# Expert stage of a streaming encoder layer: the weights stream past stationary activations as fp32r parts, and GpSimd loads x

## What is computed

```python
def expert_block(args):
    xblk, e = args
    hdn = jax.nn.silu(xblk @ w_gate_e[e]) * (xblk @ w_up_e[e])
    return hdn @ w_down_e[e]
```

## Time and profile before

| | |
|---|---|
| median of 3 runs | 2809.85 us (2809.2 to 2811.21) |
| profiled execution | 2812.55 us, span 2811.0 us |
| PE busy | 2419.6 us, 86% |
| PE weight loads | 1997.4 us, 71% |
| DVE busy | 888.5 us, 32% |
| ACT busy | 640.4 us, 23% |
| POOL busy | 168.7 us, 6% |
| HBM read, written | 301.60 MB, 74.39 MB |

### The profile page before, as it was taken

The page is one execution under the profiler, slowest core; times in us unless marked ns, Lnnn a source line. Parts: engine busy times, 40 slices in busy tenths (PEclk is TensorE's granted clock), DMA queues, the critical chain, the costliest instruction groups (busy, mean ns, idle before and its releaser), DMA issues. The chain is left out here.

```text
span 2811.0 us, 38540 instructions
## 1 busy us (share of the span) xinstructions
PE 2419.6 (86%) x14272; PEld 1997.4 (71%) x14272; DVE 888.5 (32%) x1415; ACT 640.4 (23%) x1073; POOL 168.7 (6%) x175
## 2 busy tenths in 40 slices
PE   4678979888797988899999599899279999999992
PEld 3566867667686766899888499845168877888772
DVE  5345354544535453211456432111400000000003
ACT  3133232332322221211465331111000101101010
POOL 0111010110101000000111100000200000000002
PEclk9888999999999975899999899999589999999996
DMA  3211120202111010310555431150568888888875
GB/s 90 59 39 32 46 77 0 77 1 77 31 46 55 0 55 4 121 45 28 150 177 165 139 103 45 52 193 0 187 217 327 309 318 326 326 327 314 313 291 201
DMA packets 237268, 376.83 MB, mean 134 GB/s; under 512 B 17840, under 2 KB 125656, under 8 KB 237176
## 3 DMA queue, kind: packets, MB, share of 16 engines
q1 hardware_dynamic: 216008, 302.26, 31.6%
q0 software_dynamic: 17600, 61.18, 6.8%
q10 hardware_dynamic: 3584, 12.58, 1.1%
HBM read 301.60 MB, written 74.39 MB: 134 GB/s over the span
## 5 line engine op out<-in xcount | busy, mean ns | idle before, releaser
L1715 PEld LDWEIGHTS e_gate_ps<-e_xT,e_gate 128*128 128x128 f32 x2048 | 236.0, 194 | 17.1 <-issue 17.1
L1715 PE MATMUL e_gate_ps<-e_xT,e_gate 128*128 128x96 f32 x2048 | 235.5, 276 | 1.1 <-DVE e_xT L1752 1.1
L1715 PE MATMUL e_up_ps<-e_xT,e_up 128*128 128x96 f32 x2048 | 233.9, 275 | 0.0
L1715 PEld LDWEIGHTS e_up_ps<-e_xT,e_up 128*128 128x128 f32 x2048 | 231.3, 192 | 0.0
L1726 PE MATMUL e_y_ps<-e_down,e_hT 128*96 128x512 f32 x512 | 227.4, 597 | 0.0
L1763 DVE TENSOR_TENSOR e_hT<-e_act,e_up_ps 128x384 f32<-128x384 f32 x32 | 17.7, 553 | 649.4 <-PE e_up_ps L1715 649.4
L1252 DVE COPY probsT<-turn_ps 128x512 f32<-128x512 f32 (+4 forms) x232 | 131.5, 567 | 249.0 <-PE turn_ps L1022 225.0
L101 PE MATMUL proj_ps<-w_qkv_hi,xh 128*128 128x384 f32 x544 | 194.3, 357 | 9.3 <-PEq L285 9.3
L1042 PEld LDWEIGHTS out_ps<-v_new,probsT 128*128 128x128 f32 x1152 | 156.9, 207 | 61.5 <-DVEq L84 45.0
L1152 ACT ACTIVATE probs_s<-scores,neg_max 128x256 f32<-128x256 f32 (+7 forms) x128 | 95.1, 743 | 445.6 <-DVEq L84 445.1
L1042 PE MATMUL out_ps<-v_new,probsT 128*128 128x64 f32 x1152 | 177.1, 294 | 21.2 <-DVEq L84 20.2
(11 more groups left out here) (344 smaller groups left out, 4093.2 us busy)
## 6 DMA issues: line engine op xcount, KB each, us to landing
e_gate<-w_gate_e SPq DMA_DIRECT2D x32, 2048.0 KB, 9.3
e_up<-w_up_e SPq DMA_DIRECT2D x32, 2048.0 KB, 15.1
e_down<-w_down_e SPq DMA_DIRECT2D x32, 2048.0 KB, 13.5
slot_x<-zrows POOLq DMA_DIRECT2D x48, 440.0 KB, 6.4
e_x<-slot_x SPq DMA_DIRECT2D x33, 384.0 KB, 13.0
w_qkv<-w_in SPq DMA_DIRECT2D x24, 512.0 KB, 9.8
slot_y<-e_y ACTq DMA_DIRECT2D x32, 384.0 KB, 6.1
slot_y<-zrows POOLq DMA_DIRECT2D x24, 352.0 KB, 9.6
```

Source lines behind the costliest of these rows:

```text
L1715: last = te.matmul(out[:, f * CAP:(f + 1) * CAP], weights[u][:, k, f * P:(f + 1) * P], xT[:, k, :], start=(k == 0), stop=(k == KT - 1))
```

## The change

The weights of an expert are now loaded as 6 pieces of 1 MiB, 128 x 2048 values: pieces 0 and 1 are gate, 2 and 3 up, 4 and 5 down. Each has one raw buffer. ACT rounds each piece into a high part (`high`), DVE subtracts to get the low part (`low`), both into a ring of 3 slots, and PE multiplies each piece with 12 matmuls of 512 columns (4 slices, three products each) with x or the hidden values as the stationary operand, in parts too. The gate and up results now lie as rows by hidden columns, so the hidden values are turned on PE (4 transposes, `turn_h`) before the down product. The order of the pieces on ACT, DVE and PE is 0, 1, 2, 3 of block b, then 4, 5 of block b-1. SP issues only the weight loads: a piece of the next block when the piece in the same raw buffer has been split. x and y have one buffer each. The load of x is issued by GpSimd on its own queue, after it has waited for the turn of the x before it. A loop body is one block, where it was two.

The loads of the second set of weights in `route` are gone with `second`, all 6 pieces of the first expert are loaded in `merge`. The gate and up sources are read as two rows together, 4 KiB for a partition, and x is turned in the column order that fits this. The semaphores of `normalize` and `forget_gates` come from a stack that is closed before `attend`, and SP clears each of them once at the start of `attend`.

```diff
-                w.load_in(sp, g, 0, 0)
-                w.load_down(sp, g, 0, 0)
+                for c in range(PIECES):
+                    w.load(sp, g, c, 0)
...
-                w.load_in(sp, g, 1, 1)
-                w.load_down(sp, g, 1, 1)
...
+PIECES, PIECE, RING = 6, 2048, 3
...
+        self.raw = [ctx.enter_context(nc.sbuf_tensor(f"e_raw{c}", [P, PIECE], F32)) for c in range(PIECES)]
+        self.loaded = [g.sem(f"e_loaded{c}") for c in range(PIECES)]
+    def load(self, sp, g, c, e):
+        half = slice(c % 2 * 2, c % 2 * 2 + 2)
+        if c < 4:
+            w = (g.w_gate_e, g.w_up_e)[c // 2]
+            src = w[0, bass.ds(e, 1)].rearrange("o (a p b) n -> p (o a) (b n)", p=P, b=2)[:, half, :]
+        else:
+            src = g.w_down_e[0, bass.ds(e, 1)].rearrange("o (a p) n -> p (o a) n", p=P)[:, half, :]
+        sp.dma_start(self.raw[c][:, :].rearrange("p (a n) -> p a n", a=2), src).then_inc(self.loaded[c], 16)
...
+        xb = sb("x", [CAP, D])
+        x_hi, x_lo = sb("xT_hi", [P, KT, CAP], F32R), sb("xT_lo", [P, KT, CAP], F32R)
...
+        w_hi, w_lo = ([sb(f"w_{part}{u}", [P, PIECE], F32R) for u in range(RING)] for part in ("hi", "lo"))
...
             @block.sync
             def _(sp):
                 n = sp.value_load(passes[0:1, 0:1], **limits)
-                def load_x(b, u):
-                    sp.dma_start(xb[u][:, :], g.slot_x[bass.ds(b * CAP, CAP), :]).then_inc(x_loaded[u], 16)
-                load_x(0, 0)
-                load_x(1, 1)
-                with sp.Fori(0, n - 1) as i:
-                    for u in range(2):
-                        b = i * 2 + u
-                        e = sp.value_load(expert_of[0:1, bass.ds(b + 2, 1)], min_val=0, max_val=EXPERTS - 1)
-                        sp.wait_ge(x_turned, b + 2)
-                        load_x(b + 2, u)
-                        sp.wait_ge(up_ready, b + 1)
-                        w.load_in(sp, g, u, e)
-                        sp.wait_ge(y_ready, b + 1)
-                        w.load_down(sp, g, u, e)
-                sp.wait_ge(x_turned, n * 2)
-                load_x(n * 2, 0)
+                with sp.Fori(0, n * 2 - 1) as i:
+                    e = sp.value_load(expert_of[0:1, bass.ds(i + 1, 1)], min_val=0, max_val=EXPERTS - 1)
+                    for c in range(PIECES):
+                        split = i * PIECES + (c + 1 if c < 4 else c + 1 + PIECES)
+                        sp.wait_ge(wh_ready, split)
+                        sp.wait_ge(wl_ready, split)
+                        alone(sp, g)
+                        w.load(sp, g, c, e)
+            @block.gpsimd
+            def _(pool):
+                def load_x(b):
+                    pool.dma_start(xb[:, :], g.slot_x[bass.ds(b * CAP, CAP), :]).then_inc(x_loaded, 16)
+                n = pool.value_load(passes[0:1, 0:1], **limits)
+                load_x(0)
+                with pool.Fori(0, n * 2) as i:
+                    pool.wait_ge(x_turned, i + 1)
+                    alone(pool, g)
+                    load_x(i + 1)
             @block.tensor
             def _(pe):
                 te = nc.tensor
+                def turn_x(b):
+                    pe.wait_ge(x_loaded, b * 16 + 16)
+                    alone(pe, g)
                     for k in range(KT):
+                        wide = xb[:, k // 2 * 2 * P:(k // 2 + 1) * 2 * P].rearrange("c (q b) -> c b q", b=2)
+                        last = te.transpose(xT_ps[:, k // 4, (k % 4) * CAP:(k % 4 + 1) * CAP], wide[:, k % 2, :], g.ident[0:CAP, 0:CAP])
                     last.then_inc(x_turned, 1)
...
+                def piece(c, u, at):
+                    pe.wait_ge(wh_ready, at + 1)
+                    pe.wait_ge(wl_ready, at + 1)
+                    alone(pe, g)
...
+                        last = product(nc, out, parts, (w_hi[u][:, cols], w_lo[u][:, cols]), k == 0, k == last_k)
+                    last.then_inc(w_used, 1)
+                def inner(b, later):
+                    pe.wait_ge(xh_ready, b + 1)
+                    pe.wait_ge(xl_ready, b + 1)
+                    alone(pe, g)
+                    if later:
+                        pe.wait_ge(act_ready, b)
+                        alone(pe, g)
+                    piece(0, 0, b * PIECES)
+                    if later:
+                        turn_h(b - 1)
+                    piece(1, 1, b * PIECES + 1)
+                    piece(2, 2, b * PIECES + 2)
+                    piece(3, 0, b * PIECES + 3)
+                def outer(b, u, at):
+                    pe.wait_ge(hh_ready, b + 1)
+                    pe.wait_ge(hl_ready, b + 1)
+                    alone(pe, g)
+                    pe.wait_ge(y_kept, b + 1)
+                    alone(pe, g)
+                    piece(4, u, at)
+                    piece(5, u + 1, at + 1)
...
                 turn_x(0)
+                inner(0, False)
+                turn_x(1)
+                pe.wait_ge(w_used, RING + 4)
+                pe.sem_inc(w_used, 2)
+                with pe.Fori(0, n * 2 - 1) as i:
+                    inner(i + 1, True)
+                    turn_x(i + 2)
+                    outer(i, 1, i * PIECES + PIECES + 4)
+                turn_h(n * 2 - 1)
+                outer(n * 2 - 1, 0, n * (2 * PIECES))
             @block.scalar
             def _(act):
+                sc = nc.scalar
+                def high(c, u, b, at, ringed=True):
+                    act.wait_ge(w.loaded[c], b * 16 + 16)
+                    if ringed:
+                        act.wait_ge(w_used, at + 1)
+                    alone(act, g)
+                    sc.copy(w_hi[u][:, :], w.raw[c][:, :]).then_inc(wh_ready, 1)
...
+                def silu(b):
+                    act.wait_ge(w_used, b * PIECES + RING + 2)
+                    sc.activation(act_sb[:, :], gate_ps[:, :], ACT.Silu).then_inc(act_ready, 1)
+                def keep_y(b, used):
+                    act.wait_ge(w_used, used + RING)
+                    act.wait_ge(y_stored, b * 16 + 32)
+                    alone(act, g)
+                    sc.copy(y_sb[:, :], y_ps[:, :]).then_inc(y_kept, 1)
+                def store_y(b):
+                    act.wait_ge(y_kept, b + 2)
+                    alone(act, g)
+                    act.dma_start(g.slot_y[bass.ds(b * CAP, CAP), :], y_sb[:, :]).then_inc(y_stored, 16)
+                def step(b, later):
+                    at = b * PIECES
+                    high(0, 0, b, at)
+                    high(1, 1, b, at + 1)
+                    high(2, 2, b, at + 2)
+                    if later:
+                        keep_y(b - 2, at)
+                    high_h(b - 1)
+                    high(3, 0, b, at + 3)
+                    silu(b)
+                    if later:
+                        store_y(b - 2)
+                    high(4, 1, b - 1, at + 4)
+                    high(5, 2, b - 1, at + 5)
+                    high_x(b + 1)
...
+                high_x(0)
+                for c in range(3):
+                    high(c, c, 0, c, ringed=False)
+                high(3, 0, 0, 3)
+                silu(0)
+                high_x(1)
+                act.wait_ge(wh_ready, 4)
+                act.sem_inc(wh_ready, 2)
+                step(1, False)
+                with act.Fori(0, n * 2 - 2) as i:
+                    step(i + 2, True)
...
             @block.vector
             def _(dve):
+                v = nc.vector
+                def low(c, u, at, ringed=True):
+                    dve.wait_ge(wh_ready, at + 1)
+                    if ringed:
+                        dve.wait_ge(w_used, at + 1)
+                    alone(dve, g)
+                    v.tensor_tensor(w_lo[u][:, :], w.raw[c][:, :], w_hi[u][:, :], ALU.subtract).then_inc(wl_ready, 1)
...
+                def hidden(b):
+                    dve.wait_ge(act_ready, b + 1)
+                    dve.wait_ge(w_used, b * PIECES + RING + 4)
+                    alone(dve, g)
+                    v.tensor_tensor(h_sb[:, :], act_sb[:, :], up_ps[:, :], ALU.mult).then_inc(h_ready, 1)
...
+                for c in range(3):
+                    low(c, c, c, ringed=False)
+                low(3, 0, 3)
+                hidden(0)
+                low_x(1)
+                dve.wait_ge(wl_ready, 4)
+                dve.sem_inc(wl_ready, 2)
+                with dve.Fori(0, n * 2 - 1) as i:
+                    at = i * PIECES + PIECES
+                    low(0, 0, at)
+                    low(1, 1, at + 1)
+                    low(2, 2, at + 2)
+                    low_h(i)
+                    low(3, 0, at + 3)
+                    low(4, 1, at + 4)
+                    low(5, 2, at + 5)
+                    hidden(i + 1)
+                    low_x(i + 2)
...
```

More of the change, by code:

```diff
@@ L878, in _ @@
                 load_past_k(0)
+                for done in g.early:
+                    sp.sem_clear(done)
                 store_kv(0)
@@ L1699, in turn_x, with turn_h @@
                     last.then_inc(x_turned, 1)
+                def turn_h(b):
```

(83 more changed lines are left out.)

75 lines of the change are left out of this document (24 added, 51 removed).

## The result

The changed kernel takes 3062.11 us (median of 4 runs, 3061.78 to 3066.44) beside 2810.53 us of the kernel before. The ratio is 1.0894, 95% interval 1.0874 to 1.0913. It is slower by 252 us.

What follows compares the result with a forecast made beforehand. PE was taken to bound the expert stage at 22.02 us a block, transfers close behind. Start, 30 periods of 32.5 us (0.2 + 21.1 + 11.2) and the last block gave 329 us more: 3139 us, forecast 3080 to 3215, whole range 2975 to 3215.

Steps and rivals of the forecast that it cites:

- What the loads wait for: SP's load of piece 4 waits for that piece's late split, with later loads behind it; the period exceeds 22.02 us.
- Step 2: Transfers of the six pieces and x after the issue of load 4: 20.1 and 1.0, sum 21.1 us.
- the lower bound: Low end for the transfers, 18.0 us: six pieces at 423 GB/s, 14.9 us, and a fixed part of 3.1 us.
- Step 3: From the landing of piece 3 to the split of piece 4, through PE, ACT and DVE: 11.2 us.
- Table loads: On ACT, two loads a block; the one ahead of Silu puts 1.28 us into the chain.
- rival (d): Each ACT table switch adds a drain of about 1380 ns: 3180 us, chance 2 in 100.
- The sum: Period of a block: 0.2 us to SP's issue, 21.1 for transfers, 11.2 from landing to split, 32.5 us.
- rival (a): Slower by less: the ring with warm clock, one table load or faster transfers; 3049 or 2974 us, chance 27 in 100.
- the ring: Issue of load 4, six transfers, split of piece 3, split of piece 4, next load 4: period 32.5 us.
- The signs: Expected profile: load 4 after DVE's low part, DMA near 0 about 13 us, clock 0.50, two table loads, period about 32.5.
- Rival (c): The ring does not bind and bytes set a period of 18.3 us: faster, 2705 us, chance 3 in 100.
- Rival (b): PE stays at 1.2 GHz: 33.3 us of PE, period about 34.5 us, 3199 us, chance 5 in 100.

Runs made afterwards that it cites:

- e1_order: Changed kernel with SP's loads put in the order in which their buffers are split, nothing else changed: 2703.49 us, ratio 0.9611 to the kernel before.
- e11_two_products: e1_order without the third product (low part of the stationary operand by high part of the weights), so less exact: 2684.8 us.
- e7_act_off: Changed kernel with one unread 128x2048 copy a block added on ACT at the end of its step, behind the high part of the next x: 3068.3 us.
- e6_x_behind_3: Changed kernel with x loaded by SP behind load 3 of each block instead of by GpSimd: 3032.2 us.
- e8_act_on: Changed kernel with one unread 128x2048 copy a block added on ACT between the y store and the high part of piece 4: 3090.6 us.
- e5_warm_long: Changed kernel with 38 unread matmuls after piece 5 filling PE's idle time in each block: 3006.8 us.
- e3_x_on_sp: Changed kernel with x loaded by SP behind load 5 of each block, GpSimd doing nothing in the stage: 3046.9 us.

## Why the prediction was right, point by point

- *What bounds the kernel now.* Before the change it was PE, with the transfers close behind. e1_order and e11_two_products fit both: with 17.9 us of work on PE the period went to 17.94, and no lower than 17.74 when PE's work went down by 5.6.
- *PE's work falls to 17.8 us.* Confirmed by e1_order, where PE is busy all the time and the period is 17.94. (Half of 1.54 us is 0.77, not 0.82, for the turn of x; the sum stays at 17.8.)
- *ACT and DVE.* A cast of 2048 columns took 1.906 us for 1.89, a subtraction 2.291 for 2.28. Neither bounds: 1.9 us more on ACT left the period at 30.10 (e7_act_off), and DVE is busy 43.61 of 50 us in e1_order, where the period is 17.94.
- *What the loads wait for.* Right, and shown by e1_order, in which the order alone was changed. This is the mechanism that the forecast rests on.
- *Step 2, the transfers.* The step was mis-sized by 1.1 us. By its terms the first cast starts 13.1 us after the issue of load 4 (21.1 less 8.1 for three pieces, and 0.1), and it starts 11.98 us after it. The slope of 2.58 us for one MB came from an up load with rows of 2 KiB, a down load with rows of 4 KiB and a store of y. Pieces with rows of 4 KiB now take 2.55 / 1.0486 = 2.43. That is 0.5 us for the three pieces and x (3.54 MB), the rest lies in the fixed part, about 3.3 us for 3.9. For the fixed part of 3.1 us in the lower bound the prediction showed no row; it was near. x took 0.9 us for the 1.0 in the sum (e6_x_behind_3).
- *Step 3.* Piece 0 on PE began 4.46 us after the first cast (4.4 in the sum). From there to the cast of h it was 5.49 (4.9 + 0.4 + 0.1 = 5.4). Behind it the sum goes by the casts of h and of piece 3 on ACT, but PE's piece 1 ended last. The low clock was worth 2.0 us (1.8 in the bounds).
- *Table loads.* Wrong. The prediction put one ahead of Silu in every block. The groups of ACT's line L1781 (count, busy us, mean ns, idle before) show one load in the whole stage:

```profile
L1781 ACT ACTIVATE e_act<-e_gate_ps 96x512 f32<-96x512 f32 x32 | 19.1, 596 | 15.6 <-PE e_gate_ps L103 15.6
...
L1781 ACT ACT_TABLE_LOAD x1 | 1.3, 1283 | 0.0
```

The only load stands ahead of the first Silu, which the changed kernel has in front of its loop:

```profile
2062.51 1.28 ACT L1781 ACT_TABLE_LOAD   x1
2063.80 0.60 ACT L1781 ACTIVATE e_act<-e_gate_ps 96x512 f32<-96x512 f32 x1
```

That Silu is the only function of the loop that needs a table does not explain it, since this holds for the kernel before as well, and there the load was repeated for each pair of blocks (from 2050 to 2767):

```profile
L1739 ACT ACT_TABLE_LOAD x15 | 19.2, 1283 | 12.3 <-ACT e_y L1742 12.3
```

In that kernel the loop's own first instruction is the Silu, and nothing in front of the loop loads its table. So what fits both kernels is the place of the first use, in front of the loop or in it, but no run tests it, and the cause stays open. The loop of the earlier trace rows, from which I took the pattern, uses several tables in turn. The drain of rival (d) is not seen either: Silu starts 0.01 us after the load's end (2062.51 + 1.28 = 2063.79), and there is no second load to pay for.
- *From the cast of piece 3 to load 4.* I had 9.1 us, and 7.71 were measured. The missing table load is 1.28 of it. The rest agrees only since two errors nearly cancel: Silu waits 0.49 us for PE's piece 1, which the sum did not have, and Silu and the store hold ACT for 0.77 us, where the sum had 0.6 + 0.8.
- *The sum.* 32.5 us were forecast, 30.02 measured. 30 times the 2.5 us are 75 us. The first load 4 came at 2088.3 instead of 2093, and the last block took 25.4 us to the first gather instead of 28.3. Together 82 us, which is 3096.3 - 3014.45. The time of 3062 lies below the forecast proper (3080 to 3215, 63 in 100), in the part of the whole range that belongs to rival (a) (27 in 100): the ring with the table load missing and faster transfers, which is what (a) named. Its price at 29.5 us a period was 3049.
- *The signs.* Load 4 follows the low part of piece 4, SP waits for DVE, the clock is at 0.50 at the head of the block, and DMA is near 0 for some 12 us but for the store of y: these four were right. The period was 30.02 us for about 32.5. The two table loads a block were wrong. Rival (c) fell with SP's timeline. Rival (b) fell too: the clock came back during piece 0 or, in the slowest blocks, with the first matmuls of piece 1.

## What to carry to other kernels

Where one queue issues the loads of several buffers, write down the order in which the buffers come free and put the loads in the same order. A load that stands in front of others and waits for a later event makes a ring out of the whole pipeline, and small things in that ring (the clock, the bytes of x, the place of Silu) then show in the time, though not always at their full length (e8_act_on). When a kernel gets slower and no engine is busy for most of the time, look at the queue that issues before you look at the engines.

## What the runs showed of the hardware that I had not expected

- The clock stayed at 1.00 for longer after the last matmul than in the earlier trace rows: PE's last matmul ended at 2515.4, and the clock was still 1.00 in 2518:2520 and 0.51 in 2520:2522, some 4.7 us later. In the earlier trace rows the last matmul ended at 1585.5 and the clock was 0.63 in 1588:1590. How long piece 0 then ran at the low clock differed from block to block: over the last 25 blocks it was 4.6 to 6.1 us from its first matmul to the cast of h in the changed kernel, and 3.4 in e5_warm_long.
- Pieces with rows of 4 KiB in DRAM landed 2.55 us apart, those with 2 KiB 2.71 us, one MiB each.
- A subtraction with two inputs in SBUF took 2.28 to 2.30 us in each of its 192 instances, while GpSimd issued one load of x a block in the same stage, and the same in e3_x_on_sp, where GpSimd did nothing there.
